# Where the shift's product with the first chunk's weights is made: TensorE's small products, or a sum on VectorE

## The chip, the cores and the metric

The kernel runs on one core of one Trainium2 chip. Its metric is the device time of one execution in microseconds; a value is the median of several executions. In the traces PE is TensorE, PEld its weight load, DVE VectorE, ACT ScalarE, POOL GpSimd and SP SyncE.

## The reference, cut to what matters

Two transformer blocks on 512 tokens of 1024 features, everything in f32. Four times the same front end comes before a large weight matrix: an RMS norm over the features, times `1 + scale`, plus `shift`, where scale, shift and gate are products of a vector `c` with modulation weights.

```python
shift, scale, gate = ada_mod(c, ada_w, ada_b, 3)
h = rms_norm(x, norm_g) * (1 + scale) + shift
out = h @ w
return x + gate * y
```

In the order of the work: a gated layer (`w_in`, a mix over tokens, `w_out`), then shared keys and values (`w_kv`, with a norm over each key head), then a dilated attention (`w_in`, `w_out`), then a second block with attention (`w_in`, `w_out`) and a gate/up/down layer (`w_gate`, `w_up`, `w_down`). Since `h = r * (g * x) + shift` with one `r` per token, `h @ w = r * ((g * x) @ w) + shift @ w`: the last term is one number for each output feature.

## The kernel before, in words

Features lie on the partitions, in eight tiles `x[:, m, :]` of 128 features by 512 tokens. Weights come in chunks of 128x2048 f32: eight input tiles (`kt`) by 256 output features. SyncE loads them by DMA into two buffers `w_raw[par]`; a load into a buffer waits until the low part of the chunk two before was made (`lo_done`). ScalarE copies the high part into `w_hi` (L685), VectorE subtracts to get the low part `w_lo` (`to_lo`, L1237), and TensorE makes three products, hi x hi, hi x lo and lo x hi, for each input tile and each half of 128 output features (`columns`, with the product itself in the helper `mm`, L2175). Activations are split in the same way (`x_rest`, `h_split`).

In front of three stages a chunk is multiplied before its norm is known, the "raw chunk" (`raw_chunk`, called at L2382, L2596 and L2769): i = 0 is `W_KV`, both halves, the first two key heads; i = 1 is `W_Q2`, one half, in the second block; i = 2 is `W_GU1`, both halves, gate and up. It takes `x * gain`, so it neither has the norm `r` nor the shift. After its second input tile TensorE adds the squares for the norm over the partitions (`add_squares`); later VectorE multiplies by `r` (`rescale`) and the shift's part `w_shift` is added. GpSimd meanwhile sums the squares of the x tiles (L635).

The shift's part before: VectorE splits the eight shift columns into high and low (`shift_split`, into `sh_pair`, called at L1514, L1778 and L1980). TensorE multiplies them with `w_hi` and `w_lo`, with four small products behind each of the first four input tiles and eight behind each of the next two (`shift_bias`: 32 products of two columns for i = 0, 16 for i = 1; for i = 2 the shift is the stationary side and there are 16 products of two rows and 256 columns, which ScalarE copies, `shift_row`, and four instructions turn into columns, `shift_turn`). VectorE adds the pair of columns into `w_shift` (`shift_sum`).

Every engine works in the order in which its program is written. VectorE's order around stage 0 stands at L1513 to L1560: for each of the eight tiles of the gated layer's output two units of modulation weights (`ada_out_units`, which read `ada_out` as it lands), the low part of the next chunk, a split, two more units, and the update of x (`update_x`, `x<-acc,mods,x`). The last turn, m = 7, makes the low part of `W_KV`'s first chunk. Behind it come the norm, `h_split`, `add_bias` and `gain(2)` (the bias and the gain of the next layer's modulation), `shift_sum(0)`, the two `rescale`, `key_shifted(0)` and `(1)`, and the norm of the keys (`square_rest`, `newton`). Stages 1 and 2 have the updates of the layer before in a loop over four chunks c and two halves (L1777 to L1800, L1979 to L2000).

Of the kernel before, what the change touches and what calls it, by code (L numbers as in the profile page):

```python
# [26 lines left out]
P = 128  # L27
# [127 lines left out]
def program(nc, d):  # L155
# [31 lines left out]
    take(8 * KB)  # L187
    stat2, sh_pair = at("stat2", [P, 3, 2, 2], take(64)), at("sh_pair", [P, KT, 2], take(64), F32R)
    off_wlo[1] = place(128)
# [36 lines left out]
    idle = at("idle", [P, TOK], T[7], F32R)  # L226
    sh_row = at("sh_row", [2, 2 * P], T[2])
    sq_a = [at("sq_a0", [P, TOK], T[2]), at("sq_a1", [P, TOK], T[6])]
# [138 lines left out]
    hx_start = sem("hx_start")  # L367
    xghi_done, xglo_done, shift_ready = sem("xghi_done"), sem("xglo_done"), sem("shift_ready")
    bias_done, bias_ready, pre_normed = sem("bias_done"), sem("bias_ready"), sem("pre_normed")
    sh_row_out, sh_turned = sem("sh_row_out"), sem("sh_turned")  # L370
    v_sums_done, v_stat_dve, v_stat_act = sem("v_sums_done"), sem("v_stat_dve"), sem("v_stat_act")
# [101 lines left out]
    with block:  # L473
# [203 lines left out]
        def _(act):  # L677
# [26 lines left out]
            def h_round(e, shift, dilate, kts=range(KT), h=h_hi):  # L704

                for kt in kts:
# [3 lines left out]
                                         bias=mods[:, shift + kt:shift + kt + 1]).then_inc(hhi_done, 1)  # L710

            def shift_row(n):

                act.wait_ge(bias_done, 3)
                nc.scalar.activation(sh_row[:, 0:n * P], AD[0:2, 0:n * P], ACT.Copy).then_inc(sh_row_out, 1)

# [369 lines left out]
            for kt in range(KT):  # L1086
                act.wait_ge(hx_done, 8 * 4 + kt + 1)
                src, shift = hx[kt % 2][:, :], mods[:, SHIFT_2 + kt:SHIFT_2 + kt + 1]
                nc.scalar.activation(h_hi[:, kt, :], src, ACT.Identity, bias=shift).then_inc(hhi_done, 1)
                nc.scalar.activation(f_full[:, kt, :], src, ACT.Identity, bias=shift).then_inc(full_done, 1)  # L1090
                if kt == 2:
                    shift_row(2)
            act.preload_act_table_set("silu_and_others")
# [130 lines left out]
        def _(dve):  # L1224
# [135 lines left out]

            def shift_split(i, shift):

                ge(dve, bias_done, i)
                nc.vector.tensor_scalar(sh_pair[:, :, 0:1], mods[:, shift:shift + 8].unsqueeze(2), 1.0, None, ALU.mult).then_inc(shift_ready, 1)
                dve.wait_ge(shift_ready, 2 * i + 1)
                nc.vector.tensor_tensor(sh_pair[:, :, 1:2], mods[:, shift:shift + 8].unsqueeze(2), f32(sh_pair[:, :, 0:1]), ALU.subtract)\
                    .then_inc(shift_ready, 1)

            def shift_sum(i, n):

                if i == 2:
                    dve.wait_ge(sh_turned, 1)
                    nc.vector.tensor_copy(w_shift[:, 0:n], AD[:, 2 * P:2 * P + n]).then_inc(bias_ready, 1)
                else:
                    dve.wait_ge(bias_done, i + 1)
                    sums = AD[:, 0:2 * n].rearrange("p (h e) -> p h e", e=2)
                    nc.vector.tensor_reduce(w_shift[:, 0:n], sums, AX, ALU.add).then_inc(bias_ready, 1)

# [133 lines left out]

            gain(1, SCALE_KV, G_KV, 1)  # L1513
            shift_split(0, SHIFT_KV)  # L1514
            for m in range(KT):
                u, par = divmod(W_OUTA + m, 2)
                ada_out_units(m, (0, 1))
                to_lo(*next_chunk(u, par))
# [12 lines left out]

            add_bias(FIRST_MODS + C2_UNIT, NMOD)
            gain(2, SCALE_B, G_B, 1)
            shift_sum(0, 2)
# [11 lines left out]
            key_shifted(0)  # L1546
            key_shifted(1)
            square_rest(2, sq_hi_k[1], sq[1], sq_lo_k[1])
            for half in range(2):
# [227 lines left out]
            gain(3, SCALE_1, G_LN1, 2)  # L1777
            shift_split(1, SHIFT_1)  # L1778
            nc.vector.memset(gate_one[:, :], 1.0).then_inc(fgate_dve, 1)
            for c in range(4):  # L1780
# [4 lines left out]
                for half in range(2):  # L1785
                    update_x(2 * c + half, G[2 * (w % 2) + half][:, :], GATE_B, 2 * w + half + 1, 1, True)
                    if 0 < 2 * c + half < KT - 1:
                        x_rest(1, 2 * c + half - 1)
                if c < 3:
                    to_lo(*divmod(w + 2, 2))  # L1790
# [188 lines left out]
            gain(4, SCALE_2, G_LN2, 2)  # L1979
            shift_split(2, SHIFT_2)  # L1980
            for c in range(4):
                w = W_OUT2 + c
                for half in range(2):
                    update_x(2 * c + half, G[2 * (w % 2) + half][:, :], GATE_1, 2 * w + half + 1, 1)
                    if half == 0 and c > 0:
                        x_rest(2, 2 * c - 1)
                if c < 3:
                    to_lo(*divmod(w + 2, 2))
# [184 lines left out]
        def _(pe):  # L2173
# [52 lines left out]

            def shift_bias(i, par, halves, kts):

                pe.wait_ge(shift_ready, 2 * i + 2)
                wh = w_hi[par][:, :].rearrange("p (k n) -> p k n", k=KT)  # L2230
                wl = w_lo[par][:, :].rearrange("p (k n) -> p k n", k=KT)
                for kt in kts:
                    if i == 2:
                        mm(AD[0:2, 0:256], sh_pair[:, kt, :], wh[:, kt, 0:256], kt == 0, False)
                        last = mm(AD[0:2, 0:256], sh_pair[:, kt, :], wl[:, kt, 0:256], False, kt == KT - 1)
                        continue
                    for half in range(halves):
                        s, out = slice(P * half, P * half + P), AD[:, 2 * half:2 * half + 2]
                        mm(out, wh[:, kt, s], sh_pair[:, kt, :], (kt, half) == (0, 0), False)
                        last = mm(out, wl[:, kt, s], sh_pair[:, kt, :], False, (kt, half) == (KT - 1, halves - 1))  # L2240
                if kts[-1] == KT - 1:
                    last.then_inc(bias_done, 1)

            def shift_turn(halves):

                pe.wait_ge(sh_row_out, 1)
                for half in range(halves):
                    last = mm(AD[:, 2 * P + half:2 * P + half + 1], sh_row[:, P * half:P * half + P], ones[0:2, 0:1], True, True)
                last.then_inc(sh_turned, 1)

            def raw_chunk(i, w, halves, hi, lo_kt, freed, k, norm, sq=sq):
# [521 lines left out]
            for kt in range(KT):  # L2773
                h_ready(4, kt)
                for half in range(2):
                    last = columns(G[2 + half][:, :], 1, half, KT, h_hi, h_lo_of, (kt,))
                    if kt == KT - 1:
                        last.then_inc(mm_done, 1)
                if kt == 0:
                    shift_turn(2)  # L2780
            for f in range(2, FF_GROUPS[0][2]):
# [197 lines left out]
```

## Time and profile before

| what | us |
|---|---|
| median of 3 runs | 1365.48 (1365.33 to 1367.78) |
| the profiled execution | 1366.88 |
| its span in the trace | 1365.1 |
| busy in it: TensorE / VectorE / ScalarE / GpSimd | 1357.1 / 1057.6 / 721.8 / 50.9 |

The profile is of one execution. Its span is the time from the first to the last recorded instruction. A busy share is that of the whole span, and a modelled end of a pipelined product can make TensorE look busy while it waits. In a timeline each line is one instruction: the start in us from the span's start, its duration, the engine, the line of the program (often that of a helper), the operation, output and inputs by the program's names, and in brackets the idle time of the engine just before it and what ended it. An instruction without brackets followed its predecessor closely.

### The profile page before, as it was taken

The page shows a single profiled execution, that of the slowest core. Times are in us where ns is not written, and L with a number is a line of the kernel's source. Part 1 is how long each engine was busy: PE and PEld are TensorE (multiplying, and loading weights), DVE is VectorE, ACT ScalarE, POOL GpSimd, SP SyncE. Part 2 cuts the span into 40 slices and gives each one's busy share as a digit, 9 for nine tenths or more (in the row PEclk, how much of TensorE's full clock was granted, in tenths as well). Part 3 has the DMA queues.
Part 4 walks back from the last instruction along what each step waited for, and adds up shares of the span by engine and source line. Part 5 has one row for each costly group of instructions (what it writes and reads, how often), then busy time and mean ns, then how long its engine had stood idle before and what let it go on. Part 6 is the DMA issues. An engine that isn't in the chain of part 4 may idle for free.

```text
span 1365.1 us, 21414 instructions
## 1 busy us (share of the span) xinstructions
PE 1357.1 (99%) x7911; PEld 1166.2 (85%) x7911; DVE 1057.6 (77%) x1775; ACT 721.8 (53%) x1276; POOL 50.9 (4%) x55
## 2 busy tenths in 40 slices
PE   8999999999999999999999999999999999999999
PEld 6998888888889878888888787787687998998997
DVE  7976777777799788888888868878867965983883
ACT  6744233333357566656664567766746642662561
POOL 0000000000100000000001100000030000000000
PEclk9999999999999999999999999999999999999999
DMA  9995444557743211111221231111122232333232
GB/s 377 385 380 187 168 175 182 184 206 270 290 166 109 92 63 63 62 63 62 83 72 62 93 124 63 64 61 63 59 97 71 85 131 78 105 121 124 72 116 91
DMA packets 35351, 181.51 MB, mean 133 GB/s; under 512 B 4154, under 2 KB 4922, under 8 KB 20931
## 3 DMA queue, kind: packets, MB, share of 16 engines
q1 hardware_dynamic: 34050, 177.95, 35.8%
q10 hardware_dynamic: 1216, 2.44, 0.6%
q8 instruction: 52, 0.85, 0.3%
q14 instruction: 33, 0.26, 0.1%
HBM read 177.74 MB, written 2.11 MB: 132 GB/s over the span
## 4 chain that ended last, share of the span: by engine, by line
PE 97%; DVE 1%; ACT 1%; DMA 1%; issue 0%; SPq 0%; DVEq 0%; ACTq 0%
PE acc L2175 74%; PE turn L2798 7%; PE ada L2175 3%; PE turn L2175 3%; PE norm L2175 2%; PE ada L2798 2%; PE acc L2798 2%; PE norm L2798 2%; PE turn L2641 1%; PE turn L2487 1%; DMA x<-in_x 1%; DVE ada_up L1229 0%; DVE w_lo L1237 0%; DVE s L1844 0%; ACT sq_first L738 0%
## 5 line engine op out<-in xcount | busy, mean ns | idle before, releaser
L2175 PE MATMUL acc<-h_hi,w_hi 128*128 128x512 f32 x696 | 277.7, 399 | 0.0
L2175 PE MATMUL acc<-h_hi,w_lo 128*128 128x512 f32 x696 | 272.0, 391 | 0.0
L2175 PE MATMUL acc<-h_lo,w_hi 128*128 128x512 f32 x696 | 271.2, 390 | 0.0
L1237 DVE TENSOR_TENSOR w_lo<-w_raw,w_hi 128x2048 fp32r<-128x2048 f32 x58 | 136.4, 2352 | 31.1 <-ACT w_hi L685 31.0
L2175 PEld LDWEIGHTS acc<-h_hi,w_lo 128*128 128x128 f32 x696 | 130.6, 188 | 28.4
L2175 PEld LDWEIGHTS acc<-h_hi,w_hi 128*128 128x128 f32 x696 | 130.9, 188 | 26.5 <-issue 0.4
L2175 PEld LDWEIGHTS acc<-h_lo,w_hi 128*128 128x128 f32 x696 | 131.0, 188 | 25.5
L685 ACT ACTIVATE w_hi<-w_raw 128x2048 fp32r<-128x2048 f32 x60 | 114.5, 1908 | 29.0 <-PE acc L2175 28.2
L1229 DVE SCALAR_TENSOR_TENSOR x<-acc,mods,x 128x512 f32<-128x512 f32 x48 | 38.7, 814 | 68.8 <-PE acc L2175 68.7
L2175 PE MATMUL acc<-wv_hi,h_hi 128*128 128x256 f32 x320 | 90.1, 283 | 0.0
L2175 PE MATMUL acc<-wv_lo,h_hi 128*128 128x256 f32 x320 | 88.7, 278 | 0.0
L2175 PE MATMUL acc<-wv_hi,h_lo 128*128 128x256 f32 x320 | 87.9, 278 | 0.0
L691 ACT ACTIVATE y<-norm,eps_tile 128x512 f32<-128x512 f32 x54 | 37.2, 689 | 63.7 <-PE norm L2175 63.7
L2175 PE MATMUL acc<-gu_lo,w_hi 128*128 128x512 f32 x176 | 68.5, 389 | 0.0
L2175 PE MATMUL acc<-gu_hi,w_hi 128*128 128x512 f32 x176 | 68.5, 389 | 0.0
L2175 PE MATMUL acc<-gu_hi,w_lo 128*128 128x512 f32 x176 | 68.5, 389 | 0.0
L2175 PEld LDWEIGHTS acc<-wv_hi,h_hi 128*128 128x128 f32 x320 | 60.6, 189 | 0.2
L2175 PEld LDWEIGHTS acc<-wv_lo,h_hi 128*128 128x128 f32 x320 | 60.1, 188 | 0.2
L2175 PEld LDWEIGHTS acc<-wv_hi,h_lo 128*128 128x128 f32 x320 | 59.6, 188 | 0.0
L1229 DVE SCALAR_TENSOR_TENSOR ada_out<-ada_out,csil 128x1024 f32<-128x1024 f32 x32 | 38.4, 1221 | 18.3 <-DMA ada_out<-in_ada 18.0
L2175 PE MATMUL acc<-y_hi,w_hi 128*128 128x512 f32 x128 | 50.2, 392 | 0.0
L2175 PE MATMUL acc<-y_hi,w_lo 128*128 128x512 f32 x128 | 49.9, 390 | 0.0
(385 smaller groups left out, 3483.4 us busy)
## 6 DMA issues: line engine op xcount, KB each, us to landing
w_raw<-in_weights SPq DMA_DIRECT2D x102, 1024.0 KB, 4.9
ada_v<-in_ada SPq DMA_DIRECT2D x32, 512.0 KB, 6.5
ada_raw<-in_ada SPq DMA_DIRECT2D x32, 512.0 KB, 5.6
ada_out<-in_ada SPq DMA_DIRECT2D x32, 512.0 KB, 6.5
ada_up<-in_ada_first SPq DMA_DIRECT2D x8, 1024.0 KB, 17.0
w_raw<-in_weights SPq DMA_DIRECT2D x4, 768.0 KB, 4.3
x<-in_x SPq DMA_DIRECT2D x2, 1024.0 KB, 5.9
w_first<-in_weights SPq DMA_DIRECT2D x4, 512.0 KB, 15.6
```

Of the source, the lines that this page charges most:

```text
L685: nc.scalar.activation(weights_at(u, par)[0][:, 0:used], w_raw[par][:, 0:used], ACT.Copy).then_inc(hi_done, 1)
L691: nc.scalar.activation(y0[:, :], total, ACT.Ln, scale=1.0 / count, bias=eps_col).then_inc(ln_done, 1)
L1229: return nc.vector.scalar_tensor_tensor(out, in0, scalar, in1, op0, op1, **more)
L1237: nc.vector.tensor_tensor(lo[:, 0:used], w_raw[par][:, 0:used], f32(hi[:, 0:used]), ALU.subtract).then_inc(lo_done, 1)
L2175: return nc.tensor.matmul(out, lhsT, rhs, start=start, stop=stop)
L2487: turned = nc.tensor.transpose((T0, T1)[c % 2][:, P * b:P * b + P], s_b[tile][:, lo:lo + P], ident)
L2641: turned = nc.tensor.transpose(T0[:, P * b:P * b + P], s_2[n % 3][:, 0, P * b:P * b + P], ident)
L2798: last = nc.tensor.matmul(out, w_part[:, n, :], a_part[:, n, :], start=start and n + m == 0, stop=stop and n + m == 5, skip_group_check=no ...
```

## The change

VectorE now sums, over the eight input tiles, the raw f32 weights times the shift column of that tile into one tile `fold` (`fold_shift`: one product with a column, then seven multiply-and-adds, each of which waits for the one before); it reads `w_raw`, so it waits for that chunk's load. TensorE sums `fold` over the partitions with one fp32 product with a column of ones for each half (`shift_columns`), behind the second input tile of the raw chunk and before the squares of the norm. VectorE copies the result (`shift_sum`). `shift_split`, `shift_bias`, `shift_row` and `shift_turn` are gone. The fold stands at the start of the turn m = 7 for i = 0 (256 features), and behind the update of (c, half) = (2, 0) for i = 1 (128 features) and i = 2 (256 features). `add_bias` and `gain(2)` move from before `shift_sum(0)` to behind `key_shifted(1)`. `fold` takes a free scratch tile, T[8].

```diff
-            def shift_split(i, shift):
...
+            def fold_shift(i, w, shift, n):
+
+                raw = w_raw[w % 2][:, :].rearrange("p (k n) -> p k n", k=KT)
+                dve.wait_ge(w_loaded[w % 2], 16 * (w // 2))
+                for kt in range(KT):
+                    column = mods[:, shift + kt:shift + kt + 1]
+                    if kt == 0:
+                        nc.vector.tensor_scalar(fold[:, 0:n], raw[:, kt, 0:n], column, None, ALU.mult).then_inc(shift_folded, 1)
+                    else:
+                        dve.wait_ge(shift_folded, KT * i + kt)
+                        nc.vector.scalar_tensor_tensor(fold[:, 0:n], raw[:, kt, 0:n], column, fold[:, 0:n], ALU.mult, ALU.add).then_inc(shift_folded, 1)
...
             def shift_sum(i, n):
...
+                dve.wait_ge(bias_done, i + 1)
+                nc.vector.tensor_copy(w_shift[:, 0:n], AD[:, 0:n]).then_inc(bias_ready, 1)
...
             gain(1, SCALE_KV, G_KV, 1)
-            shift_split(0, SHIFT_KV)
             for m in range(KT):
                 u, par = divmod(W_OUTA + m, 2)
+                if m == KT - 1:
+                    fold_shift(0, W_KV, SHIFT_KV, 2 * P)
                 ada_out_units(m, (0, 1))
...
-            add_bias(FIRST_MODS + C2_UNIT, NMOD)
-            gain(2, SCALE_B, G_B, 1)
             shift_sum(0, 2)
...
             key_shifted(1)
+            add_bias(FIRST_MODS + C2_UNIT, NMOD)
+            gain(2, SCALE_B, G_B, 1)
...
-            shift_split(1, SHIFT_1)
...
+                    if (c, half) == (2, 0):
+                        fold_shift(1, W_Q2, SHIFT_1, P)
...
-            shift_split(2, SHIFT_2)
...
+                    if (c, half) == (2, 0):
+                        fold_shift(2, W_GU1, SHIFT_2, 2 * P)
...
-            def shift_bias(i, par, halves, kts):
...
+            def shift_columns(i, halves):
+
+                pe.wait_ge(shift_folded, KT * i + KT)
                 for half in range(halves):
-                    last = mm(AD[:, 2 * P + half:2 * P + half + 1], sh_row[:, P * half:P * half + P], ones[0:2, 0:1], True, True)
-                last.then_inc(sh_turned, 1)
+                    last = mm(AD[:, half:half + 1], fold[:, P * half:P * half + P], ones[:, 0:1], True, True)
+                last.then_inc(bias_done, 1)
...
                     if kt == 1:
+                        shift_columns(i, halves)
                         add_squares(k, norm, sq)
-                    if kt < 6:
-                        shift_bias(i, w % 2, halves, ((0,), (1,), (2,), (3,), (4, 5), (6, 7))[kt])
```

## Rows read from the trace of the kernel before

**Rows 1.** The profile's page: busy us (share of the span) and instructions of each engine.

```profile
PE 1357.1 (99%) x7911; PEld 1166.2 (85%) x7911; DVE 1057.6 (77%) x1775; ACT 721.8 (53%) x1276; POOL 50.9 (4%) x55
```

**Rows 2.** Timeline of TensorE, first key/value chunk: start us, us, engine, line, what, [idle before].

```profile
389.31 0.39 PE L2175 MATMUL acc<-h_hi,w_hi 128*128 128x512 f32 x1
...
390.68 0.17 PE L2175 MATMUL ada<-sh_pair,w_hi 128*128 128x2 f32 x1
...
391.04 0.49 PE L2175 MATMUL acc<-h_hi,w_hi 128*128 128x512 f32 x1
```

**Rows 3.** Timeline of VectorE, just before the first key/value chunk.

```profile
384.28 1.22 DVE L1229 SCALAR_TENSOR_TENSOR ada_out<-ada_out,csil 128x1024 f32<-128x1024 f32 x1 [2.22 <-DMA ada_out<-in_ada]
...
386.72 2.28 DVE L1237 TENSOR_TENSOR w_lo<-w_raw,w_hi 128x2048 fp32r<-128x2048 f32 x1
```

**Rows 4.** Stretch, length, busy (x) of PE, PEld, DVE, ACT, POOL, clock, DMA, GB/s.

```profile
390.00:430.00 40.00, 40.00 (x239) 34.87 (x238) 38.36 (x52) 26.96 (x30) 0.00 (x0) 1.00 0.29 97
```

**Rows 5.** Tile w_raw, 377 to 379 us: its DMA issue, and issue to landing.

```profile
L485 SPq DMA_DIRECT2D w_raw<-in_weights x1: 332/332/332, 378.1 to 378.1; - x1
...
DMA to landing us min/median/max: 4.9/4.9/4.9
```

**Rows 6.** Timeline of GpSimd: two additions of squares.

```profile
382.81 1.30 POOL L635 TENSOR_TENSOR sq_sum<-sq_sum,sq_a 128x512 f32<-128x512 f32 x1 [9.51 <-ACT sq_a L730]
...
738.82 1.33 POOL L635 TENSOR_TENSOR sq_sum<-sq,sq 128x512 f32<-128x512 f32 x1 [6.25 <-ACT sq L730]
```

**Rows 7.** Timeline of VectorE: beside the second addition, and an operation on 128x256.

```profile
738.92 3.38 DVE L1237 TENSOR_TENSOR w_lo<-w_raw,w_hi 128x2048 fp32r<-128x2048 f32 x1
...
826.24 0.48 DVE L1229 SCALAR_TENSOR_TENSOR s<-s,lam_inv 128x256 f32<-128x256 f32 x1
```

**Rows 8.** Timeline of VectorE, 413 to 428 us.

```profile
413.08 0.21 DVE L1271 TENSOR_TENSOR mods<-mods,vecs 128x48 f32<-128x48 f32 x1
413.20 0.17 DVE L1229 SCALAR_TENSOR_TENSOR gscale<-mods,vecs 128x8 f32<-128x8 f32 x1
...
420.48 0.69 DVE L1292 TENSOR_TENSOR sq_lo_k<-sq,sq_hi_k 128x512 fp32r<-128x512 f32 x1 [0.50 <-ACT sq L702]
...
423.01 0.68 DVE L1229 SCALAR_TENSOR_TENSOR y_half<-norm,y_half 128x512 f32<-128x512 f32 x1
423.73 0.69 DVE L1229 SCALAR_TENSOR_TENSOR k_t<-y_half,k_t 128x512 f32<-128x512 f32 x1
...
427.96 0.69 DVE L1292 TENSOR_TENSOR sq_lo_k<-sq,sq_hi_k 128x512 fp32r<-128x512 f32 x1
```

**Rows 9.** Timeline of TensorE: the norm sums that follow those squares.

```profile
424.26 0.40 PE L2175 MATMUL norm<-sq_hi_k,ones_r 128*128 128x512 f32 x1
...
428.83 0.40 PE L2175 MATMUL norm<-sq_hi_k,ones_r 128*128 128x512 f32 x1
```

**Rows 10.** Timeline of VectorE around the first chunk of the second block.

```profile
754.17 1.18 DVE L1229 SCALAR_TENSOR_TENSOR x<-acc,mods,x 128x512 f32<-128x512 f32 x1 [1.46 <-PE acc L2175]
...
757.32 1.28 DVE L1229 SCALAR_TENSOR_TENSOR xg_lo<-x,gscale,xg_hi 128x512 fp32r<-128x512 f32 x1 [1.97 <-ACT xg_hi L723]
...
773.14 0.75 DVE L1229 SCALAR_TENSOR_TENSOR h_lo<-hx,mods,h_hi 128x512 fp32r<-128x512 f32 x1
```

**Rows 11.** Timeline of TensorE: the first product on that split tile.

```profile
774.03 0.47 PE L2175 MATMUL turn<-h_hi,wf_hi 128*128 128x512 f32 x1
```

**Rows 12.** Timeline of VectorE around the first gate/up chunk.

```profile
1011.74 0.75 DVE L1229 SCALAR_TENSOR_TENSOR x<-acc,mods,x 128x512 f32<-128x512 f32 x1 [2.75 <-PE acc L2175]
...
1013.75 2.29 DVE L1237 TENSOR_TENSOR w_lo<-w_raw,w_hi 128x2048 fp32r<-128x2048 f32 x1 [1.26 <-ACT w_hi L685]
...
1069.49 0.68 DVE L2068 TENSOR_TENSOR fast_lo<-w_raw,fast_hi 128x512 fp32r<-128x512 f32 x1
```

**Rows 13.** Timeline of TensorE: the turn products, and the first Strassen product.

```profile
1038.56 0.60 PE L2175 MATMUL ada<-ones_r,sh_row 2*128 2x1 f32 x4
...
1070.50 0.28 PE L2798 MATMUL turn<-h_hi,fast_hi 128*128 128x256 f32 x1
```

More of the change, by code:

```diff
@@ L187, in program @@
     take(8 * KB)
-    stat2, sh_pair = at("stat2", [P, 3, 2, 2], take(64)), at("sh_pair", [P, KT, 2], take(64), F32R)
+    stat2, _ = at("stat2", [P, 3, 2, 2], take(64)), take(64)
     off_wlo[1] = place(128)
@@ L226, in program @@
     idle = at("idle", [P, TOK], T[7], F32R)
-    sh_row = at("sh_row", [2, 2 * P], T[2])
+    fold = at("fold", [P, 2 * P], T[8])
     sq_a = [at("sq_a0", [P, TOK], T[2]), at("sq_a1", [P, TOK], T[6])]
@@ L367, in program @@
     hx_start = sem("hx_start")
-    xghi_done, xglo_done, shift_ready = sem("xghi_done"), sem("xglo_done"), sem("shift_ready")
+    xghi_done, xglo_done, shift_folded = sem("xghi_done"), sem("xglo_done"), sem("shift_folded")
     bias_done, bias_ready, pre_normed = sem("bias_done"), sem("bias_ready"), sem("pre_normed")
-    sh_row_out, sh_turned = sem("sh_row_out"), sem("sh_turned")
     v_sums_done, v_stat_dve, v_stat_act = sem("v_sums_done"), sem("v_stat_dve"), sem("v_stat_act")
@@ L710, in h_round @@
                                          bias=mods[:, shift + kt:shift + kt + 1]).then_inc(hhi_done, 1)
-            def shift_row(n):
-                act.wait_ge(bias_done, 3)
-                nc.scalar.activation(sh_row[:, 0:n * P], AD[0:2, 0:n * P], ACT.Copy).then_inc(sh_row_out, 1)
             def x_round(i, m, dilate=False):
@@ L1090, in _ @@
                 nc.scalar.activation(f_full[:, kt, :], src, ACT.Identity, bias=shift).then_inc(full_done, 1)
-                if kt == 2:
-                    shift_row(2)
             act.preload_act_table_set("silu_and_others")
@@ L1359, in x_rest @@
                 stt(lo, src, gscale[:, m:m + 1], hi, ALU.mult, ALU.subtract).then_inc(xglo_done, 1)
-            def shift_split(i, shift):
[L1363 to L1367, printed above, removed]
-            def shift_sum(i, n):
[L1371 to L1377, printed above, removed]
+            def fold_shift(i, w, shift, n):
[8 more added lines that the diff above has]
+                        nc.vector.scalar_tensor_tensor(fold[:, 0:n], raw[:, kt, 0:n], column, fold[:, 0:n], ALU.mult, ALU.add).then_inc(shift_folded, 1)
+            def shift_sum(i, n):
+                dve.wait_ge(bias_done, i + 1)
+                nc.vector.tensor_copy(w_shift[:, 0:n], AD[:, 0:n]).then_inc(bias_ready, 1)
             def rescale(n, acc, mm, dilate=False):
@@ L2225, in xg_lo_of @@
                 return xg_lo[m][:, :]
-            def shift_bias(i, par, halves, kts):
[L2229 to L2246, printed above, removed]
+            def shift_columns(i, halves):
+                pe.wait_ge(shift_folded, KT * i + KT)
                 for half in range(halves):
-                    last = mm(AD[:, 2 * P + half:2 * P + half + 1], sh_row[:, P * half:P * half + P], ones[0:2, 0:1], True, True)
-                last.then_inc(sh_turned, 1)
+                    last = mm(AD[:, half:half + 1], fold[:, P * half:P * half + P], ones[:, 0:1], True, True)
+                last.then_inc(bias_done, 1)
             def raw_chunk(i, w, halves, hi, lo_kt, freed, k, norm, sq=sq):
@@ L2778, in _ @@
                         last.then_inc(mm_done, 1)
-                if kt == 0:
-                    shift_turn(2)
             for f in range(2, FF_GROUPS[0][2]):
```

## The prediction

> **What bounds the kernel now.** I read the page's busy line first, then TensorE's and VectorE's timelines around the three chunks that the change touches, then the queue rows. TensorE is busy 99% of the span [rows 1], so at first sight every product taken away is time won. That is the share over the whole run. What the three stages allow is read from how long before TensorE's need each operand is ready. In the first stage (the key/value chunk) VectorE is busy 38.36 of the 40 us from 390 to 430 [rows 4], and its idle there is in a few holes before results of ScalarE. At 428.83 TensorE starts on squares whose low part VectorE began at 427.96 and finished 0.69 later, at 428.65 [rows 8, 9]. The reader is to see there two engines that arrive together: TensorE follows VectorE's result by about 0.10 to 0.14 where it plainly waits (773.14 + 0.75 = 773.89, product at 774.03 [rows 10, 11]), so the slack is 0.08 us. At 424.26 it is 0.5 (newton step 423.01 + 0.68 = 423.69). So VectorE's row of work from 384 to 428 is as long as TensorE's.
>
> **The change, part by part.**
>
> *Small products, stage 0.* Four of them stand from 390.68 to 391.04, and the next large product takes 0.09 longer than usual to start, so 0.36 to 0.45 per four [rows 2]; there are 32, eight fours: 2.9 to 3.6, I take 3.3. In stage 1 there are 16 of the same, half of it, 1.6. In stage 2 there are 16 of another shape and the four turn products, which take 0.53 (1038.56 and 0.60 long [rows 13]); at the same price 1.8 and 0.5. Added are two fp32 column products (one in stage 1); the turn products are the nearest rows, with 2 rows of weights instead of 128: two of them are four instructions, 0.53. They take over what the turn cost. TensorE's own work falls by some 2.8 + 1.4 + 1.8 = 6.0 us. That is what would come if nothing else were late.
>
> *The fold on VectorE, stage 0.* Eight instructions on 128x256, each waiting for the one in front. The nearest row has the same operation, size and a column scalar: 0.48 (826.24 [rows 7]). A VectorE instruction that needs the result in front starts 0.04 after its end (423.01 + 0.68 = 423.69, next at 423.73 [rows 8]). Eight times 0.52 is 4.2; the first has one tensor input and is shorter and the last overlaps with what follows, so 3.9. If the waits cost nothing and instructions overlap, 3.2 is the lower end; 4.2 the upper.
>
> *When it can start.* VectorE is free at 384.28 - 2.22 = 382.06 and waits for the modulation weights until 384.28 [rows 3]. That hole is the cover. But the fold reads the raw chunk, which was issued at 378.1 and landed 4.9 later [rows 5], at 383.0. And GpSimd adds squares from 382.81 [rows 6]. At 738.82 it did the same addition, and a low-part subtraction that began at 738.92 took 3.38 instead of 2.28 [rows 3, 6, 7]: it was held until about 740.0, 1.2 after the addition began. The same here holds the fold until 384.0, if its first instruction is held as well; if only the seven with two inputs in SBUF are, it ends 0.4 earlier. By the first the fold ends at 387.9, by the second at 387.5, without the collision at 383.0 + 3.9 = 386.9.
>
> The Trainium skill (SBUF — State Buffer, Who interferes with whom) says that VectorE and GpSimd share one port pair under an exclusive lock, that an instruction with two SBUF inputs or in a two-port mode needs it, and that the later one waits for the whole of the other. The two rows agree with it. By the rule the first instruction would be held too and the fold end at 387.9; by a reading in which the engines share bandwidth it would end near 387.
>
> *What stands behind the fold* on VectorE: two modulation units (2.44, from 384.28 to 386.72), the low part of the key/value chunk (2.28), which TensorE needs to begin. Before, that was ready at 389.0 and TensorE began at 389.31 [rows 2, 3]. Now it is ready at 387.7 + 2.44 + 2.28 = 392.4, so TensorE stands still for about 3.1 us. It gets 2.8 back on the small products that are gone. VectorE gets nothing back: it is 3.4 late (0.1 less where the second unit waited for its own load), has no hole until the last tile of the split, and everything to 428 hangs on it. The moved pair (bias and gain, 413.08 to 413.4, so 0.3 [rows 8]) stood in its row; behind the two shifted keys it falls into the 0.50 in which VectorE waits for ScalarE at 420.48 [rows 8]. That wait itself moves with VectorE, so the pair is hidden and 0.3 comes back, and some 0.2 in the other holes. At 427.96 VectorE is about 2.9 late, TensorE 0.08 less: **stage 0 costs 2.8 us**. From there TensorE has nothing to catch up with.
>
> The wait for the fold on TensorE comes some 7 us after its end and costs nothing; behind it stand the squares of the norm. The raw buffer is released by the low part as before, 3.4 later; its next load is wanted only after the split, some 20 us on.
>
> *Stage 1.* The fold is on 128x128, so between half of the above and all of it, some 3.0. It falls on the hole of 1.46 before the update at 754.17 and the next of 1.97 at 757.32 [rows 10], 3.43 together: hidden; uncovered it would cost what is over, 0 to 0.5. TensorE's 1.4 are not won: it already waits at 774.03 for VectorE's first split tile, and each further tile comes at VectorE's pace. That row of work hangs on the norm's squares, which now come after 0.3 for the column product and before 0.1 to 0.2 for the two small ones of the first tile: **+0.1 us**.
>
> *Stage 2.* The fold (3.9) stands before the update at 1011.74 with 2.75 idle, and 1.26 idle before 1013.75 [rows 12]: 4.0, just covered. TensorE's 1.8 shorten the chunk, but the squares of the norm come 0.3 later (0.5 for the columns, 0.2 less for the pair of the first tile), and from them hang the split, the next chunks' low parts and the first Strassen part, made at 1069.49 + 0.68 = 1070.17; TensorE takes it at 1070.50 [rows 12, 13], slack 0.2. So 1.8 of work gone becomes 1.8 of waiting: **0.0 us**, from -0.2 to +0.4. ScalarE's copy of the shift row goes too; it stood in ScalarE's waits on VectorE.
>
> **Sum.** 2.8 + 0.1 + 0.0 = +2.9 us. The profiled execution had a span of 1365.1 and 1366.88 in all, 1.8 around the span; the sum puts it at 1368.0 and 1369.8. The median of the runs shown is 1365.48, 1.4 below that execution: 1368.4.
>
> **Rivals.**
> 1. *The fold is cheaper or does not meet GpSimd.* It starts at 383.0 or its instructions overlap: it ends between 386.2 and 386.9 and stage 0 costs 1.3 to 2.1. 1367.3. For it: GpSimd's addition starts only 0.2 before the load lands, and the order could turn. Against: then GpSimd would take its turn between two of the eight.
> 2. *Not slower: the hole of 2.22 covers the fold.* It decides at 384.3: only if the fold ends by then is VectorE in time, and the slack of 0.08 at 428.83 lets TensorE neither gain nor lose: 1365.5. Against it: the load lands at 383.0, 1.3 before.
> 3. *TensorE is the bound in all three stages*, as 99% busy says, and VectorE's margins are wider than I read them: 6 us less, 1359.5. Against it: the slack of 0.08 and the plain wait at 774.03.
> 4. *The clock falls.* TensorE stands still 3 us where it never did before; the granted clock is 1.00 in this stretch [rows 4]. At its lower level, 1.2 GHz, a product takes twice as long; if that lasts for the 13 us chunk, up to 13 more, else little: 1372 as a middle. The Trainium skill (TensorE: Matmul & The Clock Gate, Part 1) says that an idle TensorE falls to the lower level; no run here shows it.
>
> **How the numbers follow.** Forecast 0.60 (its own range 1367.7 to 1369.3), rival 1 0.23, rival 2 0.06, rival 3 0.07, rival 4 0.04. About 0.2%, 2.7 us, is what can be told from no change. The forecast lies on that edge: three quarters of it above (0.45), rival 4 above, rival 1 with 0.01: slower 0.50. Same: the rest of the forecast, rival 1 and 2, 0.43. Faster: 0.07. The range reaches down to rival 2, and 0.5 below it because TensorE may keep part of the 3.2 of stages 1 and 2, and up over an upper fold of 4.2 with a held first instruction: 1365.0 to 1370.0.
>
> **What would show it.** Right: VectorE's fold starts after the chunk lands and near the end of GpSimd's addition; TensorE stands still before the first key/value product for about 3 us; at 428 plus 3 it again starts right after VectorE's low part; it waits before the split tiles in stage 1 and before the chunks behind the raw one in stage 2. Wrong: a fold that ends by 384.5, no wait of TensorE before that chunk, or a key/value stage that ends earlier than before.

## The result and the profile after

The changed kernel takes 1368.52 us in the median (1366.29 to 1371.28, 17 runs), the kernel before 1365.68 beside it; the ratio is 1.0019, with a 95% interval from 1.0012 to 1.0027, so it is slower by some 1.6 to 3.7 us. The executions of the kernel before fall into two groups, about 2.4 us apart (1364.9 to 1366.5 and 1367.6 to 1369.1), which is why medians of a dozen runs still move by half a microsecond. The profiled execution took 1367.81, with a span of 1365.9.

Between 46 and 111 us, far ahead of the change, TensorE's products of 256 columns follow each other every 0.1133 us in ten of the fourteen traces and every 0.1178 in three (kv_late, kv_sum_left_out, gu_tail_split, told below), some 2.6 us for the stretch. In the trace of before the pace changes at 78 us, with no wait of TensorE there. That is as much as the groups are apart; whether each timed execution belongs to its group for this reason is not shown. The windows view of before, and then one line of kv_late (columns as in [rows 4]):

```profile
50.00:75.00 25.00, 25.00 (x223) 25.00 (x223) 20.80 (x34) 15.71 (x35) 0.00 (x0) 1.00 0.92 347
80.00:105.00 25.00, 25.00 (x214) 25.00 (x213) 17.92 (x25) 11.57 (x25) 0.00 (x0) 1.00 1.00 395
```

```profile
50.00:75.00 25.00, 25.00 (x215) 25.00 (x214) 21.14 (x34) 15.01 (x32) 0.00 (x0) 1.00 0.93 356
```

The page after, busy time by engine. TensorE has 58 products fewer and 4.6 us less work than in [rows 1], VectorE 10.1 more:

```profile
PE 1352.5 (99%) x7853; PEld 1160.9 (85%) x7853; DVE 1067.7 (78%) x1793; ACT 722.2 (53%) x1275; POOL 50.9 (4%) x55
```

TensorE's waits between 380 and 1080 us, after (what was waited for: us, times, longest). The same view of before has one line, of 0.2 us. All are for VectorE, and four stand where the prediction looked: the key/value chunk (1.2), the key's norm (0.4), the split tiles of stage 1 (1.6), the third gate/up chunk (1.8):

```profile
PE acc L2169 <- DVE w_lo L2016: 1.8, 1, 1.8
PE turn L2169 <- DVE h_lo L1221: 1.6, 1, 1.6
PE acc L2169 <- DVE w_lo L1229: 1.2, 1, 1.2
PE acc L2169 <- DVE w_lo L1236: 0.5, 1, 0.5
PE norm L2169 <- DVE y_half L1221: 0.4, 1, 0.4
PE acc L2169 <- DVE hk_lo L1221: 0.4, 2, 0.2
```

VectorE's timeline after, around the sum of stage 0 (it answers to [rows 3]):

```profile
378.69 0.75 DVE L1221 SCALAR_TENSOR_TENSOR x<-acc,mods,x 128x512 f32<-128x512 f32 x1
379.35 0.35 DVE L1360 TENSOR_SCALAR fold<-w_raw,mods 128x256 f32<-128x256 f32 x1
379.73 4.64 DVE L1363 SCALAR_TENSOR_TENSOR fold<-w_raw,mods,fold 128x256 f32<-128x256 f32 x7
384.29 1.22 DVE L1221 SCALAR_TENSOR_TENSOR ada_out<-ada_out,csil 128x1024 f32<-128x1024 f32 x1
...
386.57 2.29 DVE L1229 TENSOR_TENSOR w_lo<-w_raw,w_hi 128x2048 fp32r<-128x2048 f32 x1
```

GpSimd's and TensorE's timelines beside it, after; and the view of the tile fold from 379 to 385 (times in ns, minimum/median/maximum):

```profile
380.18 1.30 POOL L634 TENSOR_TENSOR sq_sum<-sq_sum,sq_a 128x512 f32<-128x512 f32 x1 [9.78 <-ACT sq_a L724]
```

```profile
388.92 0.50 PE L2169 MATMUL acc<-h_hi,w_hi 128*128 128x512 f32 x1 [1.20 <-DVE w_lo L1229]
...
391.78 0.51 PE L2169 MATMUL ada<-ones_r,fold 128*128 128x1 f32 x4
```

```profile
L1363 DVE SCALAR_TENSOR_TENSOR fold<-w_raw,mods,fold x7: 485/485/1511, 379.7 to 383.9; 128x256 f32<-128x256 f32 x7
```

The sum takes 4.94 us (379.35 to 384.29). Six of its seven additions take 0.485, one 1.511: it starts after GpSimd's addition (380.18 to 381.48) and ends 0.28 behind it. The sum begins the moment that VectorE is free, and waits for no load. SyncE's timeline after, and the landing of the first of these two loads, as the view of `w_raw` from 364 to 365 has it:

```profile
364.41 0.33 SPq L484 DMA_DIRECT2D w_raw<-in_weights  x1
...
375.48 0.33 SPq L484 DMA_DIRECT2D w_raw<-in_weights  x1
```

```profile
DMA to landing us min/median/max: 5.0/5.0/5.0
```

A load follows the low part of the chunk two before. The low part just before 375.48 (373.17, 2.29 long) is that of the last chunk of the gated layer's output, so the load at 375.48 brings the second key/value chunk. The raw chunk, which the sum reads, is the load at 364.41, and it landed at 369.4, 10 us ahead of the sum. In the trace of before the raw chunk's load is that at 367.30 and lands 4.8 later, and the load at 378.1 of [rows 5] is the second chunk's.

Stage 2 after: ScalarE's, VectorE's and TensorE's timelines ahead of the third gate/up chunk, and TensorE's products behind it:

```profile
1042.23 1.28 ACT L1085 ACT_TABLE_LOAD   x1
1043.53 1.92 ACT L1101 ACTIVATE w_hi<-w_raw 128x2048 fp32r<-128x2048 f32 x1
```

```profile
1045.47 2.29 DVE L2016 TENSOR_TENSOR w_lo<-w_raw,w_hi 128x2048 fp32r<-128x2048 f32 x1 [1.82 <-ACT w_hi L1101]
```

```profile
1047.82 0.50 PE L2169 MATMUL acc<-h_hi,w_hi 128*128 128x512 f32 x1 [1.80 <-DVE w_lo L2016]
...
1049.11 0.39 PE L2169 MATMUL acc<-h_hi,w_lo 128*128 128x512 f32 x1
...
1050.14 0.63 PE L2169 MATMUL acc<-h_hi,w_lo 128*128 128x512 f32 x1
1050.57 0.63 PE L2169 MATMUL acc<-h_hi,w_hi 128*128 128x512 f32 x1
```

The windows view of that stretch after (columns as in [rows 4]); the clock is the last column but two:

```profile
1045.00:1049.00 4.00, 2.20 (x10) 1.50 (x9) 2.96 (x2) 1.59 (x3) 0.00 (x0) 1.00 0.23 35
1049.00:1053.00 4.00, 4.00 (x13) 3.11 (x12) 2.07 (x4) 3.01 (x4) 0.00 (x0) 0.57 0.57 231
1053.00:1057.00 4.00, 4.00 (x19) 3.32 (x18) 4.00 (x3) 0.00 (x0) 0.00 (x0) 1.00 0.15 31
```

On ScalarE the high part of the chunk stands behind the table load; VectorE's low part waits for the high part, and TensorE 1.80 us for the low part. About 1.5 us after TensorE goes on, its clock is at the lower level of 1.2 GHz (0.50 granted) for 3.41 us, and products follow each other every 0.43 instead of every 0.23.

**Where the time went.** Set the traces side by side instruction by instruction: the start of a TensorE weight load less that of the same load in the trace of before, as the median over a stretch (times of before). Each column is one execution; sum_out is kv_sum_left_out. A step between two rows is what a stage cost in that execution; the first row is mostly the pace between 46 and 111 us.

```
stretch        after kv_only later_two sum_out kv_late filled tail_first gu_only later_tail split_kept
 300 to  320   -1.18   -1.35    -0.95   +1.13   +1.49  -1.23    -1.32     -1.38    -1.00     -1.17
 381 to  385   -1.76   -1.93    -1.27   +0.83   +0.95  -1.81    -1.90     -0.88    -0.85     -1.75
 429 to  445   -0.82   -0.77    -1.23   +0.27   +4.17  -0.75    -1.08     -0.82    -0.83     -0.26
 775 to  800   -0.88   -0.78    -1.27   +0.26   +4.15  -0.75    -1.14     -0.81    -0.81     -0.28
1000 to 1015   -0.65   -0.71    -0.94   +0.35   +4.37  -0.55    -0.90     -0.68    -0.47     +0.09
1049 to 1050   -0.78   -0.71    -1.09   +0.21   +4.69  -0.67    -2.95     -0.67    -2.54     -0.05
1061 to 1068   +0.86   -0.71    -1.08   +0.24   +5.83  -0.64    -2.91     +0.80    -2.53     -0.02
1150 to 1200   +0.85   -0.70    +0.26   +0.45   +5.83  +0.65    -1.20     +0.80    -1.86     +1.28
VectorE ahead of TensorE at 376 to 385, against before
                0.87    0.87    -0.11    0.01   -0.03   0.77     1.01     -0.09    -0.08      0.36
```

In the profiled execution of the change: stage 0 cost 0.94, stage 1 nothing (-0.06), stage 2 up to its third chunk -0.13, the low clock 1.64. The gated layer's output loop gave 0.58 and the second block's attention cost 0.2. That is 2.0 from 300 us to the end, of the 2.8 between the medians. Steps of stage 0 are within 0.06 where at most the place of two small instructions changed in it (later_two, gu_only, later_tail); the output loop's move by themselves (before_tail, unchanged there, gave 0.38).

### The profile page after: what moved, and what is told of

It reads as the page before. It is cut to its first block, busy times and chain, and to the rows that moved or that the text cites. A ratio compares the mean times of both kernels' runs of the same rounds, so it can differ in the third digit from the quotient of the medians.

```text
span 1365.9 us, 21315 instructions
## 1 busy us (share of the span) xinstructions
PE 1352.5 (99%) x7853; PEld 1160.9 (85%) x7853; DVE 1067.7 (78%) x1793; ACT 722.2 (53%) x1275; POOL 50.9 (4%) x55
## 4 chain that ended last, share of the span: by engine, by line
PE 86%; DVE 7%; DMA 3%; issue 2%; ACT 1%; SPq 0%; DVEq 0%; ACTq 0%
PE acc L2169 64%; PE turn L2772 7%; PE ada L2169 3%; DMA ada_out<-in_ada 3%; PE turn L2169 3%; PE norm L2169 2%; PE ada L2772 2%; PE acc L2772 2%; PE norm L2772 2%; DVE w_lo L1229 1%; PE turn L2617 1%; DVE hx L1221 1%; PE turn L2463 1%; DVE ada_out L1221 1%; DVE h_lo L1221 1%
## 5 line engine op out<-in xcount | busy, mean ns | idle before, releaser
L1221 DVE SCALAR_TENSOR_TENSOR ada_out<-ada_out,csil 128x1024 f32<-128x1024 f32 x32 | 38.3, 1222 | 14.9 <-DMA ada_out<-in_ada 14.6
```

The costliest lines, as they stand in the source:

```text
L1221: return nc.vector.scalar_tensor_tensor(out, in0, scalar, in1, op0, op1, **more)
```

## The experiments

Each run has its median, that of the kernel before beside it, and the 95% interval of the ratio, where 0.001 is 1.4 us; "low clock" counts the executions whose mean granted clock was below 1.000. In none of the 109 executions of the kernel before that ran beside these was it.

| run | median | before | ratio, 95% | low clock |
|---|---|---|---|---|
| the change | 1368.52 | 1365.68 | 1.0012 to 1.0027 | 11 of 17 |
| kv_only | 1367.57 | 1365.75 | 1.0004 to 1.0025 | 4 of 11 |
| later_two | 1367.39 | 1365.75 | 1.0002 to 1.0020 | 2 of 11 |
| kv_sum_left_out | 1366.29 | 1365.75 | 0.9986 to 1.0003 | 3 of 11 |
| kv_late | 1370.36 | 1365.75 | 1.0018 to 1.0039 | 6 of 9 |
| filled | 1367.92 | 1366.01 | 1.0005 to 1.0024 | 0 of 11 |
| tail_first | 1367.08 | 1366.01 | 0.9993 to 1.0010 | 4 of 12 |
| gu_only | 1367.92 | 1366.01 | 0.9998 to 1.0016 | 4 of 12 |
| later_tail | 1365.80 | 1366.01 | 0.9988 to 1.0008 | 0 of 12 |
| split_kept | 1368.14 | 1365.61 | 1.0012 to 1.0030 | 6 of 11 |
| gu_tail_split | 1364.90 | 1365.61 | 0.9987 to 1.0005 | 0 of 11 |
| before_tail | 1365.45 | 1365.61 | 0.9993 to 1.0011 | 0 of 11 |
| gu_tail_fill | 1366.19 | 1366.21 | 0.9985 to 1.0003 | 0 of 11 |

**kv_only** and **later_two**: the change split in two.

```diff
                     if kt == 1:
-                        shift_columns(i, halves)
+                        if i in FOLDS:                 # kv_only: (0,), later_two: (1, 2)
+                            shift_columns(i, halves)
                         add_squares(k, norm, sq)
+                    if i in OLDS and kt < 6:
+                        shift_bias(i, w % 2, halves, ((0,), (1,), (2,), (3,), (4, 5), (6, 7))[kt])
```

> The change in stage 0 alone (the sum on VectorE for the key/value chunk, and the moved bias and gain); stages 1 and 2 as before. Theory A (the two traces set side by side: TensorE came to the key/value chunk 1.76 us ahead of the trace of before, began it 0.39 ahead and left the norm of the keys 0.80 ahead, so stage 0 cost 1.0; the other 1.6 came in stages 1 and 2): 0.8 to 1.5 us over before, about 1366.8. Rival B (the prediction's split: stage 0 costs 2.8 and the others nothing): 2.3 to 3.3 over before, about 1368.5. Either way the first product of that chunk waits for VectorE's low part.

> The change in stages 1 and 2 alone; stage 0 with TensorE's 32 small products and the old place of bias and gain. Theory A: 1.3 to 2.0 us over before, about 1367.4: a wait of TensorE of 1.5 to 2 us ahead of the third gate/up chunk, behind it a stretch of 3 us in which its granted clock is below 1 and a product of 512 columns takes 0.43 instead of 0.23, so the small products that are gone are paid back in waiting and the clock is lost on top. Rival B: within 0.4 of before, about 1365.8, the same wait but no loss behind it.

Measured: 1.8 and 1.6 over before, with intervals of 0.5 to 3.4 and 0.3 to 2.7. Both parts cost; the times alone don't part A from B for kv_only and hardly for later_two. The traces do: the step of stage 0 is 0.94 for the whole change and 1.16 for kv_only, not the 2.8 of B, and later_two loses 1.20 from 1000 us on, not nothing. Four executions of kv_only had a low clock, and its trace has no other wait of more than 0.2 from 380 to 1080 us than stage 0's. later_two has the wait of 1.8 but, in its trace, no fall of the clock; it loses 1.34 behind 1068 us instead: 0.34 at the wait for the first Strassen part, and 1.0 in a slower step after it. The windows view of TensorE's 256-column products shows the step, before and later_two:

```profile
1075.00:1100.00 25.00, 25.00 (x223) 25.00 (x223) 23.68 (x42) 16.59 (x38) 0.00 (x0) 1.00 0.37 128
```

```profile
1075.00:1100.00 25.00, 25.00 (x217) 25.00 (x216) 23.68 (x42) 16.73 (x37) 0.00 (x0) 1.00 0.37 127
```

In the same 25 us TensorE, never idle and at a clock of 1.00, makes 217 products instead of 223. From one weight load to the next it is 0.1167 us there against 0.1133, all the way to the 512-column chunks at 1108.

**kv_sum_left_out**: what the sum itself costs.

```diff
-                for kt in range(KT):
+                for kt in ((KT - 1,) if i == 0 else range(KT)):
```

> The whole change, but in stage 0 VectorE makes only one of the eight instructions of the sum, so the shift's part of the first two keys is left out in all but one input tile. It shows what the other seven (4.6 us in the trace) cost in time. Theory A (they fill a hole of 2.3 us that VectorE had there anyway, and TensorE paid the rest as its wait of 1.2): 0.8 to 1.5 below the whole change, about 1367.3; stage 0 stays at VectorE's pace, so TensorE's 2.8 of removed products don't come out. Rival C (without the sum TensorE is the bound in stage 0): 3 to 4 below the whole change, about 1365.

Measured: 1366.29, 2.2 under the whole change, and the two intervals against before don't overlap: the sum does cost. It lies between A (0.8 to 1.5) and C (3 to 4). In the trace stage 0 gained 0.56 against before, not the 2.8 of its removed products. TensorE still waits there for VectorE (0.6, 0.4 and 0.4 us, its view of waits): without the sum too, stage 0 runs at VectorE's pace.

**kv_late**: the sum beyond the low part that TensorE waits for.

```diff
-                if m == KT - 1:
-                    fold_shift(0, W_KV, SHIFT_KV, 2 * P)
...
             x_rest(0, KT - 1, True)
+            fold_shift(0, W_KV, SHIFT_KV, 2 * P)
             x_norm(N_X1, 1, 1)
```

> The whole change, but the sum for the key/value chunk stands behind the last split tile of the raw chunk, beyond the low parts that TensorE waits for, and TensorE's column product behind the last input tile; the next load into that buffer waits for the sum. So TensorE does not stand still ahead of the key/value chunk. Theory A (the whole row of VectorE up to the keys' norm is as long as TensorE's, so what counts is the work in it, and here the sum of 4.0 no longer lies in the hole of 2.3 in which VectorE waits for modulation weights, though it does not meet GpSimd either): 1 to 2 over the whole change, about 1369.8. Rival D (the loss is TensorE's standstill at that chunk): 1.0 to 1.4 below the whole change, about 1367.3.

Measured: 1370.36, 1.8 over the change, as A says (the intervals against before overlap). The wait ahead of the key/value chunk is gone, and stage 0 costs 3.2 instead of 0.9: VectorE's hole is back unused, the sum stands in the full row, and TensorE waits for the split tiles. Of these 2.3 some 0.9 is the lead of VectorE that the trace of the change had and this one has not (last line of the table). kv_late, VectorE's timeline, and then the first line of TensorE's waits:

```profile
385.29 1.23 DVE L1223 SCALAR_TENSOR_TENSOR ada_out<-ada_out,csil 128x1024 f32<-128x1024 f32 x1 [2.24 <-DMA ada_out<-in_ada]
...
397.17 0.35 DVE L1363 TENSOR_SCALAR fold_kv<-w_raw,mods 128x256 f32<-128x256 f32 x1
397.56 3.61 DVE L1366 SCALAR_TENSOR_TENSOR fold_kv<-w_raw,mods,fold_kv 128x256 f32<-128x256 f32 x7
401.08 0.75 DVE L1223 SCALAR_TENSOR_TENSOR hx<-x,gscale,y 128x512 f32<-128x512 f32 x1
```

```profile
PE acc L2171 <- DVE hk_lo L1223: 3.2, 6, 2.3
```

**filled**: dummy products where TensorE stands still.

```diff
...
+                if f == 2:
+                    pe.wait_ge(acc_freed, 2 * w - 19)
+                    for _ in range(7):
+                        mm(G[2 * (w % 2)][:, :], ones_r[:, :], h_hi[:, 0, :], True, True)
```

The products ahead of the other two waits, in stages 0 and 1, are not shown.

> The whole change, with dummy products of 512 columns where TensorE stands still: 5 ahead of the key/value chunk, 7 ahead of the first split tile of stage 1, 7 ahead of the third gate/up chunk. They take no other work away and TensorE starts the real work no earlier. Theory E (of the time over before, a part is lost because TensorE's standstill is followed in some executions by 3.4 us at a granted clock of 0.50; the mean clock of a span was 1.000 in all 32 executions of the kernel before and below that in 12 of 17 of the change): a mean clock of 1.000 in nearly every execution, and a median 0.8 to 1.6 below the whole change, about 1367.3. Rival F (the clock falls for other reasons or costs nothing, since VectorE is the bound behind it): as the whole change, 1368.5, or slower by what the dummies delay.

Measured: no execution had a mean clock below 1.000, against 11 of 17 of the change (the 12 in the expectation was a miscount); so the falls do come from the standstills. The median is 1.9 over before instead of 2.8, with intervals that overlap, so a gain is not shown. In its trace, with the clock kept up, TensorE comes to the Strassen parts before VectorE's low part, waits, and then runs with the slow step (-0.64 to +0.65 in the table). One loss was put in place of the other.

**tail_first** and **later_tail**: ScalarE's high part ahead of its table load, in the change and in later_two.

```diff
                 nc.scalar.activation(h_hi[:, kt, :], src, ACT.Identity, bias=shift).then_inc(hhi_done, 1)
+                if kt == KT - 1:
+                    tail_hi(W_GU1 + 2)
                 nc.scalar.activation(f_full[:, kt, :], src, ACT.Identity, bias=shift).then_inc(full_done, 1)
...
-            tail_hi(W_GU1 + 2)
```

> The whole change, with ScalarE making the high part of the third gate/up chunk ahead of its last copy of the split activations and its table load of 1.3 us, so 1.9 earlier. Theory G (the standstill of 1.8 us ahead of that chunk is ScalarE's table load in the chain from the norm, and with it gone TensorE has the small products' 1.8 until VectorE's next row, the Strassen parts at 1070): no wait there, no fall of the clock in stage 2, a wait of some 1 us at the first Strassen product instead; 0.5 to 1.5 below the whole change, about 1367.5. Rival H (the whole of the 1.8 is waited for at the Strassen parts): no fall of the clock, 0 to 0.5 below.

> The change in stages 1 and 2 alone, stage 0 as before, with ScalarE's high part of the third gate/up chunk put ahead as in the run tail_first. Theory G: the 1.6 over before that the two later stages cost is gone and some of the removed products come out: -0.8 to +0.3 against before, about 1365.4. Rival H: still 0.8 to 1.6 over before, with a wait or slower steps of TensorE at the Strassen parts.

Measured: 1367.08 (1.1 over before, against 2.8 of the change) and 1365.80 (-0.2; later_two +1.6). The interval of tail_first (-1.0 to +1.4) includes no change and lies under that of the change (1.6 to 3.7); that of later_tail (-1.6 to +1.1) overlaps later_two's. The wait of 1.8 is gone in both traces, and from 1000 to 1049 us TensorE gains 2.05 and 2.07, where the change gains 0.13. tail_first, ScalarE's and VectorE's timelines:

```profile
1041.25 1.90 ACT L1094 ACTIVATE w_hi<-w_raw 128x2048 fp32r<-128x2048 f32 x1
1043.06 0.70 ACT L1102 ACTIVATE f_full<-hx,mods 128x512 f32<-128x512 f32 x1
1043.78 1.28 ACT L1103 ACT_TABLE_LOAD   x1
```

```profile
1043.32 2.28 DVE L2017 TENSOR_TENSOR w_lo<-w_raw,w_hi 128x2048 fp32r<-128x2048 f32 x1
```

So the table load (1.28), with the last copy (0.7) that was passed as well, was what in the chain turned stage 2's removed products into waiting. Part is given back at the wait for the first Strassen part (0.67 in later_tail's column of the table), and in tail_first the slow step takes 1.0 more.

**gu_only**: stage 2 alone.

> The change in stage 2 alone; stages 0 and 1 with TensorE's small products, the moved bias and gain at the new place. Theory I (stage 1 costs nothing, as TensorE's start of the heads' gates shows in two traces, and all of the 1.6 of the two later stages is stage 2's): 1.2 to 2.0 over before, about 1367.3. Rival J (it is split): 0.5 to 1.1 over before.

Measured: 1.9 over before in the median, with an interval of -0.3 to +2.2 that includes no change, so the times don't part I from J. Its trace has stage 1 at 0.0, the wait of 1.8, and 1.47 lost to a fall of the clock right behind it, as I says.

**split_kept**: does the removed split explain VectorE's lead?

```diff
             gain(1, SCALE_KV, G_KV, 1)
+            nc.vector.tensor_scalar(sh_pair[:, :, 0:1], columns_8, 1.0, None, ALU.mult).then_inc(shift_ready, 1)
+            dve.wait_ge(shift_ready, 1)
+            nc.vector.tensor_tensor(sh_pair[:, :, 1:2], columns_8, f32(sh_pair[:, :, 0:1]), ALU.subtract).then_inc(shift_ready, 1)
```

> The whole change, with the two small VectorE instructions of the old shift split for the key/value stage kept at their place ahead of the gated layer's output loop (0.17 each, 0.28 us of VectorE together); nothing reads their result. Theory K (removing them put VectorE 1.3 us further ahead of TensorE for that whole loop, because the second of two modulation loads then no longer ends a wait of 1.42; with that lead the sum cost stage 0 only 1 us of the 2.8 forecast): VectorE leads TensorE by about 0.3 or less at 376 us, TensorE waits 2 to 3 us ahead of the key/value chunk, and the median is 0.8 to 1.8 over the whole change, about 1369.8. Rival L (the lead is a matter of the execution's start): as the whole change, 1368.5, with the same wait of 1.2.

Measured: 1368.14, as the change. K falls, and L's wait of 1.2 did not come either: VectorE's lead went from 0.87 to 0.36 and the wait from 1.2 to 1.7, half a microsecond and not 1.3. In the trace of before VectorE waits 8 times for modulation loads in that loop, 18.0 us; here 6 times, 14.9, and in the change 6 times, 14.6. Over all traces the lead stands (0.77 to 1.01, five traces, also in gu_tail_fill with the old stage 0) where the old split is not made ahead of the loop and TensorE kept the pace of 0.1133 in the first stretch; without that split but with the slower first stretch it does not (-0.12 to 0.01, three traces), nor with the split as before (about -0.1, four traces). So both seem to take part; why is open.

**gu_tail_split**, **before_tail**, **gu_tail_fill**: a version put together, and its control.

```diff
...
+                if m == 3:
+                    shift_split(0, SHIFT_KV)
...
```

```diff
                 ge(pe, silu_second, i - 1)
+                if i == 0:
+                    for _ in range(5):
+                        mm(x_bank(i), ones_r[:, :], h_hi[:, 0, 0:256], True, True)
                 product(i, B11, x_bank(i), (h_hi, h_lo), 0, 0, True, True)
```

> A version put together from what the runs showed: stage 0 and stage 1 with TensorE's small products as before (bias and gain at the new place), stage 2 with the sum on VectorE, ScalarE's high part of the third gate/up chunk put ahead of its table load, and the small shift split of stage 0 moved from ahead of the output loop into its fourth turn, where VectorE waits for a load. Theory G with K (TensorE has stage 2's removed products and a faster way through the output loop; no standstill is left but at the Strassen parts): 0.7 to 1.5 below before, about 1364.8. Rival H: the standstill at the Strassen parts is followed by the slower step of 0.1167 instead of 0.1133 us per product of 256 columns, which takes 1 us back: within 0.4 of before.

> The kernel before, with only ScalarE's high part of the third gate/up chunk put ahead of its last copy and its table load, as in tail_first. Theory G (in the kernel before TensorE is the bound there, as it comes to that chunk 0.1 to 0.5 after its low part): within 0.4 of before, so what tail_first won is won from the wait that the change made. Rival M (the reordering is a gain by itself): 0.8 or more below before.

> The version gu_tail_split with five dummy products of 256 columns ahead of the first Strassen product, as long as TensorE's wait for its low part there (0.56 from the product before to the first one in that trace). Theory N (TensorE's slower step, 0.1167 us per product of 256 columns instead of 0.1133 over some 300 products, follows only a wait there: it stood in 5 of the 7 traces with that wait and in none of the 6 without): the step is 0.1133, and the median 0.5 to 1.0 below gu_tail_split, 0.8 to 1.6 below before, about 1364.2. Rival O (the slow step comes from something else, or the executions that were timed mostly did not have it): the step is 0.1167 again, or the median is that of gu_tail_split within 0.3, about 0.5 below before.

Measured: before_tail is the kernel before within its interval, so the reordering is worth something only where a wait was made. gu_tail_split is 0.7 below before in the median, an interval that includes no change; its trace gains 2.06 from 1000 to 1049 us and gives 1.7 back at the Strassen parts, 1.0 of it to the slow step. gu_tail_fill has the normal step in its trace, as N says, first its products and then the windows view:

```profile
1066.67 0.75 PE L2195 MATMUL turn<-h_hi,ones_r 128*128 128x256 f32 x5
1067.26 0.29 PE L2827 MATMUL turn<-h_hi,fast_hi 128*128 128x256 f32 x1
```

```profile
1075.00:1100.00 25.00, 25.00 (x223) 25.00 (x222) 23.35 (x41) 16.36 (x38) 0.00 (x0) 1.00 0.37 128
```

That execution took 1363.71, and from 1000 us to the end its trace gains 1.4 against before. Three of the eleven are below the lowest of all executions of before (1364.85). But the other eight lie from 1365.20 to 1366.65, and the median is that of before; six of them are 2.5 to 2.9 above the profiled one, about what the slower pace of the first stretch costs, and no trace shows whether they had it. So neither theory's number came out; that this version is faster is suggested by its one trace and not shown by its times.

## Why the prediction was right, and where it was not

The forecast was 1368.4 and slower, the median is 1368.52. The sum was right; its terms were not. 2.8 + 0.1 + 0.0 was put down, and by the traces it is about 1 for stage 0, nothing for stage 1, and 1.2 to 1.5 for stage 2 in six of the seven traces that have the change there and ScalarE's old order (0.1 in the seventh, kv_sum_left_out). Two errors of opposite sign met, and that the sum came so near the median is luck.

- *The duration of the sum and the hold by GpSimd* were right: 3.9 and 1.0 forecast, 3.9 measured alone (kv_late), 4.94 with the hold; 3.0 for stage 1, 3.0 measured (751.73 to 754.73). The addition that is held starts 0.07 after GpSimd's and ends 0.28 behind it, which agrees with what the Trainium skill says (SBUF — State Buffer, Who interferes with whom): the later of the two waits for the whole of the other.
- *When it can start* failed, by 1.0. The load at 378.1 [rows 5] is not that of the raw chunk but of the next one; the raw chunk had been issued at 367.30 and was in its buffer some 10 us before VectorE was free. So the sum starts when VectorE is free, 382.06 in the times of before, and nothing waits until 383.0. VectorE was 2.5 late and not 3.4. What rivals 1 and 2 say of the landing at 383.0 rests on the same reading.
- *What stands behind it* failed by a further 0.9. The trace of before shows the two engines arriving together at the key/value chunk [rows 2, 3]. VectorE's loop there goes by its loads, and in the changed kernel's trace it came 0.87 further ahead. Over the five traces with the sum at that place, what stage 0 cost and VectorE's lead add up to the same: 0.94 + 0.87, 1.16 + 0.87, 1.06 + 0.77, 0.82 + 1.01, 1.49 + 0.36, or 1.81 to 2.03. So the sum costs what it takes beyond hole and lead, as the rule of the prediction had it, with the lead put at nothing.
- *That stage 0 runs at VectorE's pace* was right, and rival 3 wrong: with the sum left out its stage gained 0.56 instead of 2.8, and with the sum moved off TensorE's way (kv_late) it cost more, 3.2 against the 1.8 to 2.0 above.
- *Stage 1* was right: 0.1 forecast, -0.06 to 0.0 in the traces, with TensorE's wait of 1.6 in place of the products.
- *Stage 2* was right as far as it went: 1.8 of removed work became a wait of 1.8, and TensorE was 0.13 ahead behind it. The step that failed is "1.8 of work gone becomes 1.8 of waiting: 0.0". A wait was priced as if it were free. In the trace of the change it was followed by 3.41 us at a clock of 0.50, which cost 1.64; with the clock kept up (filled, later_two), by a wait at the Strassen parts and the slow step, 1.3.
- Rival 4, the clock that falls, had been put at stage 0, at a chance of 0.04 and up to 13 us. It happens, in 11 of the change's 17 executions, and cost an eighth of that in the one traced, where it stood in stage 2. The Trainium skill (TensorE: Matmul & The Clock Gate, Part 1) says that an idle TensorE falls to the lower level. Here waits of 1.8 did so in the traces of after, gu_only and kv_late and not in those of later_two, kv_sum_left_out and split_kept, and dummy products in the waits left no execution with a low clock.

Open: why VectorE had its lead in some traces; what starts the slow step (it followed a wait at the Strassen parts in five traces of seven and stood in none of the six without that wait, of which gu_tail_fill makes a seventh, but in the first stretch a slower pace began in the trace of before without any wait, so a wait is not its only start); and what of the 2.8 between the medians the pace of the first stretch adds.

## What to carry to other kernels

Work taken from the engine that is busy 99% is won only up to the next operand it must wait for; read that engine's waits by stage, and the chain behind each wait, before counting the products that go. Before a landing goes into a sum, count which chunk the load carries: here the load beside the change was the next chunk's. A slack between two engines is one execution's number where one of them follows loads: read it in more than one trace. And a wait made on TensorE can have a price of its own behind it: move the chain (here a table load on ScalarE) before removing its work. By the traces that did more here than keeping TensorE busy with dummy products: from 1000 us on tail_first gained 0.3, filled lost 1.2.

## What was not expected of the hardware

- A granted clock of 0.50 for 3.41 us, 1.5 us after TensorE had gone on from a wait of 1.80; the same wait in other executions left the clock at 1.00.
- A second pace of TensorE at full clock: 0.1167 us from one 256-column weight load to the next instead of 0.1133, held for some 38 us without a gap and gone at the next change of shape; between 46 and 111 us 0.1178 in three traces, and from 78 us on in the trace of before.
